# The order of gate/up, down, combine and transposes in the expert loop of a two-layer encoder trunk

## The reference

```python
def _hier_moe(h, w_group, b_group, w_expert, b_expert, w_gate, w_up, w_down):
    ...
    for g in range(N_GROUPS):                                # 4 groups of 8 experts
        a = jnp.einsum('td,edf->tef', t, w_gate[g])          # d 1024, f 256
        u = jnp.einsum('td,edf->tef', t, w_up[g])
        act = jax.nn.silu(a) * u * combine[:, g, :, None]    # combine: 2 of 32 experts per token
        y = y + jnp.einsum('tef,efd->td', act, w_down[g])
    return y.reshape(bsz, seq, d)

        x = x + _hier_moe(h, ...)
        gate = jax.nn.sigmoid(_rmsnorm(x, norm_ple[i]) @ ple_w_gate[i])
        x = x + gate * (p[i] @ ple_w_proj[i])
```

## Time and profile before

| | |
|---|---|
| median of 3 runs | 866.68 us (863.19 to 868.13) |
| the profiled execution | 868.72 us, span 867.0 us |
| mean granted TensorE clock | 0.958 |
| TensorE busy | 777.1 us, 90% of the span |
| VectorE, ScalarE, GpSimd busy | 396.2, 237.9, 191.4 us |
| moved by DMA | 245.48 MB, mean 283 GB/s |

### The profile page before, as it was taken

How to read it: one execution, slowest core, us unless ns; L and a number is a source line. 1 busy time by engine, 2 the same in 40 slices (tenths; PEclk the granted TensorE clock), 3 DMA queues, 4 the chain that set the end, 5 groups by cost and what they waited for, 6 DMA issues and landing times.

```text
span 867.0 us, 10684 instructions
## 1 busy us (share of the span) xinstructions
PE 777.1 (90%) x4025; PEld 424.1 (49%) x4025; DVE 396.2 (46%) x720; ACT 237.9 (27%) x422; POOL 191.4 (22%) x198
## 2 busy tenths in 40 slices
PE   2677879899999998889999878998999999998997
PEld 1556744643343343336878654546434344333356
DVE  6996742723232322226678658615322232321264
ACT  3323123421111101016575444413310111110153
POOL 5874400221110110000056364002211011110000
PEclk8588979999999999999999959999999999999999
DMA  6035070999999999996787670077499999999961
GB/s 219 1 57 196 5 288 4 349 410 411 414 413 412 412 412 415 411 412 244 261 209 242 241 213 6 28 297 257 140 378 410 417 410 413 414 410 414 376 255 48
DMA packets 79524, 245.48 MB, mean 283 GB/s; under 512 B 21715, under 2 KB 22769, under 8 KB 70897
## 3 DMA queue, kind: packets, MB, share of 16 engines
q1 hardware_dynamic: 75184, 240.37, 72.1%
q0 software_dynamic: 1600, 4.26, 2.3%
q10 hardware_dynamic: 2688, 0.17, 0.2%
HBM read 243.16 MB, written 1.60 MB: 282 GB/s over the span
## 4 chain that ended last, share of the span: by engine, by line
PE 82%; DVE 7%; issue 5%; ACT 2%; POOL 2%; DMA 1%; SPq 0%; ACTq 0%; DVEq 0%; POOLq 0%
PE PS L1813 26%; PE PS L1843 13%; PE PS L1559 10%; PE PS L1853 7%; PE PS L1741 3%; PE PS L2030 3%; PE PS L1782 2%; PE PS L1683 2%; PE PS L2010 2%; PE PS L1989 2%; PE PS L1617 2%; PE PS L1937 2%; PE PS L1824 1%; POOL qrs L699 1%; PE PS L1698 1%
## 5 line engine op out<-in xcount | busy, mean ns | idle before, releaser
L1813 PE MATMUL PS<-ring,xe 128*64 128x512 f32 x1024 | 228.0, 594 | 17.6 <-issue 15.3
L1813 PEld LDWEIGHTS PS<-ring,xe 128*64 128x64 f32 x1024 | 76.9, 137 | 163.8 <-issue 163.8
L1843 PE MATMUL PS<-ring,actT 128*64 128x512 f32 x512 | 116.9, 598 | 1.7 <-DVE actT L1317 1.4
L626 POOL COPY xe<-xg 128x512 f32 x60 | 47.2, 787 | 297.6 <-PE PS L1813 288.2
L1331 DVE TENSOR_TENSOR olo<-PS,ohi 128x512 fp32r<-128x512 f32 x64 | 44.2, 691 | 123.6 <-ACT ohi L869 123.6
L1317 DVE COPY actT<-PS 128x256 f32<-128x256 f32 x32 | 13.6, 424 | 173.3 <-PE PS L1824 173.3
L869 ACT ACTIVATE ohi<-PS 128x512 fp32r<-128x512 f32 x64 | 38.3, 598 | 153.0 <-PE PS L1843 153.0
L1022 DVE SCALAR_TENSOR_TENSOR ringr<-ring,gT,dwh 128x512 fp32r<-128x512 f32 x80 | 61.9, 824 | 27.4 <-ACT dwh L740 26.2
L861 ACT ACTIVATE act<-PS 128x256 f32<-128x256 f32 x32 | 12.3, 384 | 224.0 <-PE PS L1813 224.0
L1843 PEld LDWEIGHTS PS<-ring,actT 128*64 128x64 f32 x512 | 34.7, 136 | 67.1 <-issue 67.1
L1559 PE MATMUL PS<-ringr,rawh 128*128 128x512 f32 x160 | 63.4, 396 | 0.8 <-DVE ringr L1022 0.8
(11 more groups left out here) (321 smaller groups left out, 1036.3 us busy)
## 6 DMA issues: line engine op xcount, KB each, us to landing
ring<-in_moe_w_gate SPq DMA_DIRECT2D x128, 512.0 KB, 15.8
ring<-in_moe_w_up SPq DMA_DIRECT2D x128, 512.0 KB, 17.4
ring<-in_moe_w_down SPq DMA_DIRECT2D x64, 1024.0 KB, 17.5
ring<-in_nat_w_qkv SPq DMA_DIRECT2D x6, 2048.0 KB
ring<-in_ple_w_gate SPq DMA_DIRECT2D x4, 2048.0 KB
ring<-in_s_w_out SPq DMA_DIRECT2D x2, 2048.0 KB
ring<-in_nat_w_o SPq DMA_DIRECT2D x2, 2048.0 KB
ring<-in_s_w_in SPq DMA_DIRECT2D x1, 2048.0 KB
```

The costliest lines, as they stand in the source:

```text
L626: pool.tensor_copy(xe[:, e % 4, :, :], xg[:, :, bass.ds(first, CAP)]).then_inc(S("xe_ready"), 1)
L1813: ins = mm(PS[CAP * h_:CAP * h_ + CAP, 0, :].rearrange("p (u f) -> p u f", u=2), xe[:, (2 * p + h_) % 4, k, :], wv[h_][:, k], start=k == 0 ...
L1843: ins = mm(PS[CAP * h_:CAP * h_ + CAP, 2 + n, :], actT[:, k, CAP * h_:CAP * h_ + CAP], wd[h_][:, k, 512 * n:512 * n + 512], start=k == 0, ...
```

## The change

The order of one turn of the loop, on TensorE and, to match, on VectorE. Before, turn p runs `gate_up(p)`, `act_transposes(p-1)`, `combine(p-2)`, `down(p-1)`. After, it runs `gate_up(p)`, `down(p-1)`, `combine(p-2)`, `act_transposes(p)`. Behind the loop, `act_transposes(15)` has moved into the last turn, and `down(15)` now stands ahead of `combine(14)`. No instruction is added or taken out, and the lists of ScalarE, GpSimd and SyncE are the same.

```diff
@@ VectorE, moe(i)
                 for p in range(NP):
-                    if p:
-                        actT_evict(i, p - 1)
                     gate(i, p)
                     if p + 1 < NP:
                         weights_of(i, p + 1)
+                    actT_evict(i, p)
                     if p:
                         out_lo(i, p - 1)
                     slots_of(i, p)
-                actT_evict(i, NP - 1)
                 out_lo(i, NP - 1)
@@ TensorE, moe(i)
                     gate_up(i, p, 4, KD)
                     if p:
-                        act_transposes(i, p - 1)
+                        down(i, p - 1, 0)
+                        down(i, p - 1, 1)
                     if p >= 2:
                         combine(i, p - 2)
-                    if p:
-                        down(i, p - 1, 0)
-                        down(i, p - 1, 1)
-                act_transposes(i, NP - 1)
-                combine(i, NP - 2)
+                    act_transposes(i, p)
                 down(i, NP - 1, 0)
                 down(i, NP - 1, 1)
+                combine(i, NP - 2)
```

## The result

The changed kernel takes 872.25 us (median of 10 runs, 870.32 to 877.48) against 866.02 us of the kernel before (10 runs, 863.19 to 870.21). The ratio is 1.0086, with a 95% interval of 1.0067 to 1.0106: slower by 0.9%, or 7.4 us (5.8 to 9.2). The two medians by themselves are 6.2 us apart. The forecast was 873.5 us, 6.8 us over before.

A forecast was written before the change was run, and what follows sets the result against it. The prediction took weight loads to bound the loop, leaving TensorE's work behind the last arrival to count. Loop and start cost nothing, each layer's tail +3.4 us: 866.7 + 6.8 = 873.5 us, range 869 to 878.5 us.

The forecast's parts named there:

- The sum: Whole kernel: 3.4 us more tail in each of two layers, 6.8 us, with loop and loop start at nothing.
- What bounds the kernel: In the loop, weight loads set the end, 15.2 us a turn against 12.7 us of TensorE; its order there costs nothing.
- The loop's new wait: In late turns, down waits 1.4 us for its weights; the next gate_up absorbs this, so the cost is nothing.
- The sentence on a loop without cover: In the loop, 2.6 us of uncovered copies would make turns 15.3 us against 15.2 us of loads, about nothing.
- The start of the loop: At each layer's first turns, transposes ahead of gate_up(1) may shift load releases: 0, bounds -0.7 and +0.3 us.
- The arrival of the down weights, T: Start of down(14) in the tail, 5.07 us after the last gate/up arrival, at 382.6 us in layer 0.
- The tail's two pauses: Behind the last arrival: 2.0 us before the last down, 1.4 us before the last combine; tail +3.4 us a layer.
- Which of the copies is late: In the tail, ohi's first half ready at 6.09 us after down(14) starts, bank 1's copy at 6.29, out_lo(14) behind it.
- The banks: In the tail, PSUM banks rotate soundly and are free; what speaks against the new order is the single ohi.
- Covered: Rival, chance 0.11: in the tail the copies run under the next matmul group; +1.4 us a layer, 869.5 us.
- The clock: Rival, chance 0.13: tail pauses drop TensorE's granted clock in one or both layers; 1.7 us a layer, up to 877 us.
- Hidden: Rival, chance 0.10: the ple stage waits for something other than TensorE, so the longer tail costs nothing; 865.3 to 866.7 us.

The follow-up runs named there:

- loop alone: New order in turns 0 to 14, old order in turn 15 and behind the loop, against the kernel before: ratio 1.0002, 865.54 us.
- two buffers, `out_lo` first: Changed kernel with ohi and olo doubled, and out_lo(14) ahead of the bank 1 copy on VectorE in turn 15: ratio 1.0023, 2.0 us over before.
- one line back: Changed kernel with combine(14) moved back ahead of down(15) behind the loop: ratio 1.0058, 5.0 us over before.
- two buffers: Changed kernel with two buffers each of ohi and olo, for even and odd pairs: ratio 1.0055, 4.8 us over before.
- tail alone: Kernel before, old order in turns 0 to 14, new order in turn 15 and behind the loop: ratio 1.0082, 872.60 us.
- pause filled: Changed kernel with 8 unused matmuls of ones between the last transposes and the last down: ratio 1.0095, 873.19 us.
- the run with eight fillers: Kernel before with 8 unused matmuls of ones added to every turn from 2 to 14: ratio 1.0432, 37.4 us over before.
- first profile: Profiled execution of the changed kernel, the slowest of its 10 runs: 877.48 us, span 875.8 us.
- third profile: Changed kernel without an edit, profiled again by itself: 872.87 us.
- the two measurements: Changed kernel against the kernel before, measured over 10 runs and, without an edit, again over 4 runs: ratios 1.0086 and 1.0114.

## Why the prediction was right, and where it wasn't

The sum, put against the runs:

| kernel | tail, us a layer | 2 x (tail - 18.46) | measured over before, us |
|---|---|---|---|
| loop alone | 18.3 | -0.3 | 0.2 (-1.4 to 1.7) |
| two buffers, `out_lo` first | 19.6 | 2.3 | 2.0 (0.2 to 3.7) |
| one line back | 20.5 | 4.1 | 5.0 (3.4 to 6.6) |
| two buffers | 20.7 | 4.5 | 4.8 (2.9 to 6.7) |
| tail alone | 22.2 | 7.4 | 7.1 (4.7 to 9.4) |
| pause filled | 22.2 | 7.4 | 8.2 (6.5 to 10.0) |
| the change | 22.2 to 23.9 | 7.4 to 10.9 | 7.4 (5.8 to 9.2) |

- **What bounds the kernel.** Right. The chain's 82% on TensorE is no measure for the loop; the loads set its end, and the order in it is worth nothing that could be measured (loop alone).
- **The loop's new wait.** Right: 1.3 us in front of `down` (1.4 forecast), paid back in front of `gate_up`.
- **The sentence on a loop without cover.** Wrong. It set one turn of 12.7 + 2.6 = 15.3 us against 15.2 us of loads and called that nothing. But TensorE starts the loop three pairs behind the loads and has to catch up. By the run with eight fillers, turns lengthened to 12.7 + 2.07 = 14.8 us already cost 37 us in all. The right bound is the sum of the waits. The forecast didn't use the sentence, since the cover held.
- **The start of the loop.** Not decided. Layer 1's stretch from first `gate_up` to last arrival is 0.30 us longer in the first profile (bounds -0.7 and +0.3), but in the four profiles of the changed kernel it took 199.50, 197.71, 197.91 and 199.49 us, against 199.20 in the one of before. A term of a few tenths can't be seen in that. The ratio of the loop alone holds it near nothing.
- **The arrival of the down weights, T.** 4.97 us behind the last gate/up arrival (5.07 forecast).
- **The tail's two pauses.** Right in mechanism. `down` to `down` 7.86 us (7.8 forecast), last `combine` 16.83 us behind T at its start in the profile with the fallen clock, which is 15.1 at full clock (14.7). The term was 3.4 us a layer and measured 3.7. `combine(14)` took 2.06 us where 1.9 was put, and the second pause 1.55 us where 1.4 was put, 0.1 of it as 0.14 us in place of 0.04 between `olo` and the matmul.
- **Which of the copies is late.** Half right. The text had `out_lo(14)` behind the copy on VectorE, with `ohi` ready 0.2 us before it. In the change both came within 0.03 us of each other, since `combine(13)` took 2.06 us and the transposes 0.22. The runs with two buffers show that the copy matters once `ohi` is out of the way: without that, the second buffer would have been enough.
- **The banks.** Wrong for the first pause. The prediction has the banks free, and only the single `ohi` against the new order. But `down(15)` writes into banks 2 and 3, which `out_lo(14)` had not emptied when TensorE got there: the row `PE PS L1841 <- DVE olo L1331` has this wait, 1.9 us. The banks were free for the second pause alone, where `out_hi(15)` empties banks 2 and 3 while `combine(14)` writes into 4 to 7. The sum has the right wait all the same, as it made `down(15)` wait for both halves of `olo`.
- **Covered.** The rival's tail of +1.4 us a layer is that of two buffers with `out_lo(14)` first, +1.2 us measured. The Trainium skill, in Perfetto Trace Analysis, section Matmuls, says that independent groups of matmuls should rotate through PSUM banks, so that emptying one overlaps filling the next. In the second pause that alone did not help: the banks were free, and 1.55 us of emptying still lay bare behind `combine(14)`, until `ohi` and `olo`, into which the banks are emptied, were doubled too.
- **The clock.** This had 0.13 as a rival, for one or both layers, and took place in 3 of 8 tails and two of four executions, at the forecast price of 1.7 us. So the chance was too low, and the prediction's own sign of being wrong, a clock below 1.00 between 385 and 400 us, stands in the first and the third profile. The sum left the clock out. Its average share is about 1.3 us by the estimate above, and it is 3.4 us of the 5.2 us by which the first profile lies above the median. That the time came out so near the forecast is in part luck: at full clock the tails alone give 7.4 us, with the clock's share 8.7 us, and the two measurements 7.4 and 9.9 us.
- **Hidden.** Refuted: the ple stage's L1933 follows the last `combine` without a gap, and what the tail loses comes out at the end: behind the last `combine` of layer 1 lie 35.07 us in the first profile, and 35.02 before.

What stays open: the median of the kernel with the pause filled is no lower than the change's. The intervals (6.5 to 10.0 and 5.8 to 9.2 us) leave room for the 1.3 us, but do not show it.

## What to carry to other kernels

Where a loop's end is set by loads, read a change of order at its two ends: what releases the loads at the start, and the work left behind the last arrival, where every pipeline stage that the loop covered lies bare. The order that is free in the loop can be the wrong one for the last turn, so write the last turn by itself. The slack of the loop here was the sum of the engine's waits for loads over the whole loop, not the difference between a turn's work and a turn's loads. And two groups of matmuls that write into the same banks need enough work between them for the banks to be emptied; in the last turn only 2.3 us stood between the two `down`.

## What the runs showed of the hardware

The granted clock after the same pause differs from one execution to the next. Behind 1.9 us of standstill in the tail it fell to 1.2 GHz in 3 of 8 cases, with the same instructions ahead; in the kernel with the tail alone it fell in neither of two. The gather of 32 matmuls, with a pause of 1.8 us ahead of it, took 7.50 to 10.43 us in the profiles of these kernels. Profiles of one kernel thus differ by several us with no cause in the code (spans of 867.9 and 875.8 us for the change), and two single profiles are compared stretch by stretch, not by their spans.
